# Two transformer blocks on one core: fill chunks, fin steps and index scores put in other places

## The reference

```
u = rmsnorm(h, mix_norm)
(fq, fk, fv, ff, dq, dk, dv, iq, ik, iw, mq, g) = split(u @ w_in)
o_a = fox_attention(fq, fk, fv, logf)             # 8 heads of 64, causal, with forget gates
score = sum_h iw_h * relu(iq_h . ik)              # index scores; top 128 keys for each query
o_b = dsa_attention(dq, dk, dv, ...)              # 8 heads over the chosen keys
km, vm = split(rmsnorm(mem, mem_norm) @ w_mem_kv)
o_c = memory_attention(mq, km, vm)                # 4 heads of 128 over 256 memory rows
gates = sigmoid(g)                                # 3 x 1024 columns
h = h + sum(gates * (branches @ w_branch)) @ w_out
```

## Time and profile before

| | |
|---|---|
| median of 3 runs | 2127.72 us (2126.78 to 2128.96) |
| profiled execution | 2127.72 us, its span 2125.9 us |
| TensorE busy | 1991.0 us, 94% |
| weight loads | 1613.4 us, 76% |
| GpSimd busy | 1450.9 us, 68% |
| VectorE busy | 977.3 us, 46% |
| ScalarE busy | 512.3 us, 24% |
| mean granted TensorE clock | 0.978 |

### The profile page before, as it was taken

How to read it: one execution, slowest core, us unless ns; L and a number is a source line. 1 busy time by engine, 2 the same in 40 slices (tenths; PEclk the granted TensorE clock), 3 DMA queues, 4 the chain that set the end, 5 groups by cost and what they waited for, 6 DMA issues and landing times.

```text
span 2125.9 us, 26050 instructions
## 1 busy us (share of the span) xinstructions
PE 1991.0 (94%) x8941; PEld 1613.4 (76%) x8941; DVE 977.3 (46%) x1198; ACT 512.3 (24%) x920; POOL 1450.9 (68%) x1662
## 2 busy tenths in 40 slices
PE   7999999999999989889999999999898879999996
PEld 6788888777777877777788888876677648888884
DVE  6432330687655477656432331057766573333004
ACT  3111100343444422430211110023555331111001
POOL 5777777776665656447777777776555568777771
PEclk9999999999999999999999999999999979999998
DMA  5333322332211223003333332242100113333320
GB/s 173 89 97 91 98 99 89 84 86 72 60 50 51 69 70 90 11 24 96 89 97 92 98 99 99 94 104 50 30 21 21 40 40 99 99 92 95 99 89 40
DMA packets 255460, 163.87 MB, mean 77 GB/s; under 512 B 30124, under 2 KB 245230, under 8 KB 255262
## 3 DMA queue, kind: packets, MB, share of 16 engines
q1 hardware_dynamic: 253728, 157.90, 25.4%
q10 hardware_dynamic: 1662, 5.06, 0.6%
HBM read 160.81 MB, written 2.13 MB: 77 GB/s over the span
## 4 chain that ended last, share of the span: by engine, by line
PE 76%; DVE 12%; POOL 6%; issue 3%; ACT 2%; DMA 1%; ACTq 0%; POOLq 0%; DVEq 0%; SPq 0%
PE bank L797 12%; PE bank L798 12%; PE bank L799 12%; PE bank L885 5%; PE bank L886 5%; PE bank L887 5%; PE bank L1056 4%; PE bank L1057 4%; PE bank L1058 4%; POOL w_lo L654 3%; PE bank L952 2%; DVE work L2309 1%; DVE work L2239 1%; POOL w_hi L650 1%; PE bank L1317 1%
## 5 line engine op out<-in xcount | busy, mean ns | idle before, releaser
L654 POOL TENSOR_TENSOR w_lo<-raw,w_hi 128x256 fp32r<-128x256 f32 x1192 | 953.9, 831 | 24.8
L650 POOL TENSOR_SCALAR w_hi<-raw 128x1024 fp32r<-128x1024 f32 x298 | 322.9, 1084 | 420.0 <-PE bank L799 165.1
L797 PE MATMUL bank<-u_hi,w_hi 128*128 128x512 f32 x1056 | 417.1, 395 | 16.9 <-DVE u_lo L2165 15.7
L798 PE MATMUL bank<-u_lo,w_hi 128*128 128x512 f32 x1056 | 413.8, 392 | 0.0
L799 PE MATMUL bank<-u_hi,w_lo 128*128 128x512 f32 x1056 | 413.6, 392 | 0.0
L797 PEld LDWEIGHTS bank<-u_hi,w_hi 128*128 128x128 f32 x1056 | 199.7, 189 | 66.4 <-issue 18.4
L799 PEld LDWEIGHTS bank<-u_hi,w_lo 128*128 128x128 f32 x1056 | 199.9, 189 | 42.2
L798 PEld LDWEIGHTS bank<-u_lo,w_hi 128*128 128x128 f32 x1056 | 200.1, 189 | 41.1 <-issue 0.7
L1056 PE MATMUL bank<-u_hi,w_hi 128*128 128x512 f32 x464 | 193.8, 418 | 2.3 <-DVE u_lo L2165 1.6
L885 PE MATMUL bank<-hid_hi,w_hi 128*128 (+1 forms) x480 | 187.0, 389 | 1.0 <-POOL w_lo L654 1.0
L887 PE MATMUL bank<-hid_hi,w_lo 128*128 (+1 forms) x480 | 186.8, 389 | 0.0
(11 more groups left out here) (513 smaller groups left out, 3263.4 us busy)
## 6 DMA issues: line engine op xcount, KB each, us to landing
raw<-in_w_in SPq DMA_DIRECT2D x52, 512.0 KB, 3.7
raw<-in_ffn_w_gate SPq DMA_DIRECT2D x44, 512.0 KB, 3.7
raw<-in_ffn_w_up SPq DMA_DIRECT2D x44, 512.0 KB, 3.8
raw<-in_ffn_w_down SPq DMA_DIRECT2D x44, 512.0 KB, 3.5
raw<-in_w_gate SPq DMA_DIRECT2D x22, 512.0 KB, 3.7
raw<-in_w_up SPq DMA_DIRECT2D x22, 512.0 KB, 3.7
...
```

The lines of the kernel that those rows point to most:

```text
L650: pool.tensor_scalar(w_hi[:, s, :], raw[:, k, :], 1.0, 1.0, ALU.mult, ALU.mult).then_inc(hi_done, 1)
L654: pool.tensor_tensor(w_lo[:, s, c], raw[:, k, c], w_hi[:, s, c].bitcast(F32), ALU.subtract).then_inc(low_quarter if quarter < 3 else split ...
L797: pe.matmul(outs[:, 0:n], wh, rhs_hi[:, c, :], start=(c == 0), stop=False)
L798: pe.matmul(outs[:, 0:n], wh, rhs_lo[:, c, :], start=False, stop=False)
```

## The change

It keeps all computation and moves it.

- Preparation. TensorE asks for the norm's total in unit DK instead of FG; the transposes of v go to bank 6 and to unit FG, the head sums of q0 and dk trade their banks. VectorE and ScalarE follow: the k split comes ahead of the v split, the head norm of q0 ahead of the FG copy.
- `fin` writes two work tiles in SBUF (`W[3]`, `W[4]`) instead of banks 2 and 6, and `fin_low` reads them there. The last steps (`fin_low` 4 to 7, `fin` 6 and 7) and the IQ0 copy move from memory slot 0 into `prep`.
- Memory slots. Of the filling steps, 1 instead of 3 stand behind the first score and 4 instead of 2 behind the last; 4 instead of 8 ahead of the value products.
- Fox slots. One step instead of two behind the first and the third score, two instead of one behind the third and fourth transposed score. ScalarE does `q_high` and the output copies ahead of the fifth `exps`; GpSimd splits unit u+4 between the sixth and the seventh low part.
- Gates. The index scores stand in gates 4 to 7 instead of 5 to 8.

TensorE at the start of memory slot 0, before: `L952` are its scores, `bank4` the chunks of the next panel.

```diff
--- before.py
+++ after.py
@@ -608,7 +608,6 @@
         I_BANKS = 0, 1, 6
         MEM_BANKS, FOX_BANKS = ((0,), (2, 3), (6,), 7), ((0,), (2, 3), (6, 7), None)
         AUX, Q_BANK, K_BANK = 1, 4, 5
-        FIN_BANKS = 2, 6
         USUAL = S_BANKS, T_BANKS, O_BANKS, DEN_BANK
         B2_BANKS = (0,), (2, 3), (6, 7), None
         FIRST_FILL = 7
@@ -620,7 +619,6 @@
 
             steps = [x for x, n in enumerate(n for head in FILLS for n in head) for _ in range(n)]
             return steps[k - FIRST_FILL]
-        IDX_GATES = range(5, 9)
         DQ_SUMS, DQ_TURNS = (9, 13, 17, 21), (11, 15, 19, 23)
         PV_LAG = 2
 
@@ -725,10 +723,12 @@
                     for k in (1, 2, 3):
                         low_part(A_FOX, fox_heads, steps[8 * p + k])
                     one(u + 3)
-                    for k in (4, 5, 6, 7):
+                    for k in (4, 5):
                         low_part(A_FOX, fox_heads, steps[8 * p + k])
-                    for k in (4, 5):
-                        one(u + k)
+                    one(u + 4)
+                    for k in (6, 7):
+                        low_part(A_FOX, fox_heads, steps[8 * p + k])
+                    one(u + 5)
             for u in range(RAW):
                 one(u)
             run(RAW, U_PREP)
@@ -1072,23 +1072,23 @@
                         pe.wait_ge(f_out, 7)
                         head_sum(H_K0, 6, k0_sq, ones, MEM)
                 for c in chunks(U_DK, 2, *early):
-                    if c == 4:
-                        values(VR_MEM, AUX, v0_raw, MT)
+                    if c == 2:
+                        pe.wait_ge(f_out, 8)
+                        sum_total(N_MIX, 7)
                 for c in chunks(U_FG, 3, *early):
                     if c == 1:
-                        pe.wait_ge(f_out, 8)
-                        sum_total(N_MIX, 7)
+                        pe.wait_ge(h_std, H_K0 + 1)
+                        values(VR_MEM, 6, v0_raw, MT)
+                    if c == 4:
+                        head_sum(H_Q0, AUX, q0_sq, ones)
                 for c in chunks(U_IK, 5, *early):
-                    if c == 2:
+                    if c == 3:
                         pe.wait_ge(n_std, N_MIX + 1)
-                        head_sum(H_Q0, 7, q0_sq, ones)
-                    if c == 5:
-                        pe.wait_ge(s_lo, S_MEM + 1)
-                        head_sum(H_DK, AUX, dk_sq, blk64)
+                        head_sum(H_DK, 7, dk_sq, blk64)
                 pe.wait_ge(p_raw, 1)
                 for c in chunks(U_DV, 4, *early):
                     if c == 3:
-                        pe.wait_ge(h_std, H_DK + 1)
+                        pe.wait_ge(h_std, H_Q0 + 1)
                         pe.wait_ge(p_raw, 3)
                         for i in range(TT):
                             last = pe.transpose(bank[AUX][:, i * HD:(i + 1) * HD], fg_raw[0:HD, i * P:(i + 1) * P],
@@ -1190,12 +1190,12 @@
                     pe.wait_ge(r_sin, R_PREP + i - 1)
                 for qt in range(TT):
                     scores(i, qt)
-                    go_on(panels, 1 if qt else 3)
-                go_on(panels, 2)
+                    go_on(panels, 1)
+                go_on(panels, 4)
                 for h, k, kb, t, b in steps:
                     scores_t(h, k, kb, t)
                     go_on(panels, 2)
-                go_on(panels, 8)
+                go_on(panels, 4)
                 for h, k, kb, t, b in steps:
                     values_mm(h, k, kb, b)
                     go_on(panels, 4)
@@ -1218,7 +1218,7 @@
                     values_mm(h, i, kb, b)
                 for qt in range(TT):
                     scores(2 * p, qt)
-                    go_on(panels, 2 if qt % 2 == 0 else 1)
+                    go_on(panels, 1)
                 for qt in range(2):
                     scores(2 * p + 1, qt)
                     go_on(panels, 1)
@@ -1229,7 +1229,7 @@
                     go_on(panels, 1)
                 for k in (2, 3):
                     t_of(k)
-                    go_on(panels, 1)
+                    go_on(panels, 2)
                 for k in range(4):
                     v_of(k)
                     go_on(panels, 1)
@@ -1273,10 +1273,10 @@
                     if n < 8:
                         pe.wait_ge(g_raw, 4)
                     else:
-                        pe.wait_ge(g_sig, n - 7 if n < 12 else n - 3)
+                        pe.wait_ge(g_sig, n - 7)
                     for c in chunks(U_GATE + n, 2 + n % 4, *U):
-                        if n in IDX_GATES and c >= 2:
-                            index_score(2 * (n - IDX_GATES[0]) + (c - 2) // 3, 1 + (c - 2) % 3)
+                        if n < 8 and c >= 2:
+                            index_score(2 * (n - 4) + (c - 2) // 3, 1 + (c - 2) % 3)
                         if n in DQ_SUMS and c == 3:
                             head_sum(H_DQ + DQ_SUMS.index(n), 6, W[4], blk64)
                         if n in DQ_TURNS and c == 4:
@@ -1752,7 +1752,7 @@
 
             def fin_high(c):
                 act.wait_ge(fin_t, c + 1)
-                act.activation(u_hi[:, c, :], bank[FIN_BANKS[c % 2]][:], ACT.Copy).then_inc(fin_hi, 1)
+                act.activation(u_hi[:, c, :], W[3 + c % 2], ACT.Copy).then_inc(fin_hi, 1)
 
             def prep():
                 act.wait_ge(unit_done, U_K0 + 1)
@@ -1760,22 +1760,22 @@
                 copy(k0_raw[:], bank[0][:, 0:MEM], h_raw)
                 head_std(H_K0, 6, k0_sq, P, MEM)
                 value_copy(U_V0, 1, v0_raw, MEM)
-                act.wait_ge(v_t, VT_MEM + 1)
-                copy(mst["vh"][:], bank[AUX][:, 0:MEM].rearrange("p (k n) -> p k n", k=MT), s_hi)
                 norm_std(N_MIX, b=7)
                 act.wait_ge(h_out, H_K0 + 1)
                 copy(mst["kh"][:], k0_raw[:], s_hi)
+                act.wait_ge(v_t, VT_MEM + 1)
+                copy(mst["vh"][:], bank[6][:, 0:MEM].rearrange("p (k n) -> p k n", k=MT), s_hi)
                 act.wait_ge(p_raw, 1)
                 act.activation(q0_sq[:], q0_raw[:], ACT.Square).then_inc(h_sq, 1)
                 act.wait_ge(p_raw, 2)
                 act.activation(dk_sq[:], dk[:], ACT.Square).then_inc(h_sq, 1)
                 fin_high(0)
-                head_std(H_Q0, 7, q0_sq, P)
+                head_std(H_Q0, AUX, q0_sq, P)
                 fin_high(1)
-                head_std(H_DK, AUX, dk_sq, HD)
-                load_exp()
                 act.wait_ge(h_out, H_Q0 + 1)
                 copy(mst["qh"][:], q0_raw[:], s_hi)
+                head_std(H_DK, 7, dk_sq, HD)
+                load_exp()
                 for c in range(2, 5):
                     fin_high(c)
                 act.wait_ge(iw_t, 1)
@@ -1934,12 +1934,11 @@
                     k_std()
                     forget_sums(p + 1)
                     load_exp()
+                    q_high()
                 else:
                     gate_copy(1)
+                output(2 * p)
                 exps(*steps[4])
-                if p < 3:
-                    q_high()
-                output(2 * p)
                 exps(*steps[5])
                 if p < 3:
                     v_copy()
@@ -1977,9 +1976,9 @@
 
             def later_gates():
                 for n in range(4, 24):
-                    if n in IDX_GATES:
+                    if n < 8:
                         for k in range(6):
-                            x = 6 * (n - IDX_GATES[0]) + k
+                            x = 6 * (n - 4) + k
                             cols_ = (2 + k % 3) * P
                             act.wait_ge(ix_s, x + 1)
                             if x >= 3:
@@ -2460,30 +2459,29 @@
             def fin(c):
                 if c >= 2:
                     dve.wait_ge(fin_lo, c - 1)
-                dve.scalar_tensor_tensor(out=bank[FIN_BANKS[c % 2]][:], in0=hT[:, c, :], scalar=gain[:, G_MIX + c:G_MIX + c + 1],
+                dve.scalar_tensor_tensor(out=W[3 + c % 2], in0=hT[:, c, :], scalar=gain[:, G_MIX + c:G_MIX + c + 1],
                                          in1=W[2], op0=ALU.mult, op1=ALU.mult).then_inc(fin_t, 1)
 
             def fin_low(c):
                 dve.wait_ge(fin_hi, c + 1)
-                dve.tensor_tensor(u_lo[:, c, :], bank[FIN_BANKS[c % 2]][:], u_hi[:, c, :].bitcast(F32), ALU.subtract).then_inc(fin_lo, 1)
+                dve.tensor_tensor(u_lo[:, c, :], W[3 + c % 2], u_hi[:, c, :].bitcast(F32), ALU.subtract).then_inc(fin_lo, 1)
 
             def prep_raw(u, dst_, b, r=P):
                 dve.wait_ge(unit_done, u + 1)
                 dve.tensor_tensor(dst_, bank[b][0:r, :], W[2][0:r], ALU.mult).then_inc(p_raw, 1)
 
             def prep():
-                low(S_MEM, mst["vl"][:], bank[AUX][:, 0:MEM].rearrange("p (k n) -> p k n", k=MT), mst["vh"][:])
                 head_norm(H_K0, k0_sq, k0_raw, G_MK, MEM)
                 norm_recip(N_MIX)
                 dve.wait_ge(n_rec, N_MIX + 1)
                 prep_raw(U_Q0, q0_raw[:], 4)
```

(17 more changed lines are left out.)

## The result

The changed kernel took 2145.56 us in the median (2145.09 to 2146.89, 4 runs) against 2127.8 before: the ratio is 1.0085, with a 95% interval of 1.0066 to 1.0102, so +17.8 us. Slower was forecast, but +9.3, and the time lies 3 us above the stated range. The profiled execution's span grew from 2125.9 to 2143.4, +17.5.

The account below looks back on a forecast made before the run. TensorE, busy 94% of the span, was taken as the bound, so only its waits matter. Memory slots and preparation +7.0, fox slots +1.4, gates -0.4 and clock +1.3 gave +9.3, 2137.0 us; range 2126 to 2142.5.

Parts of the forecast that it names:

- preparation, the wait for ik: Preparation: the norm's total is asked for five chunks earlier, so TensorE's 0.7 us wait for ik goes, -0.7.
- slot 0 (front 2.2, values 1.4): Memory slot 0: second score waits 2.2 us for the row maximum; value product waits for GpSimd's low part, +1.4.
- slot 3: Memory slot 3: second score +0.7; second head sum, now behind the value product, delays the fox scores, +1.6.
- A wash: Fox slots, third value product: GpSimd's 4.0 us split ends about when ScalarE releases the low part; -0.2 each in slots 0 to 2.
- The front's +0.7: Fox slots 1, 2 and 3: second score directly behind the first waits for the row maximum, 0.7 us each.
- Between -1.7 and +5; I take +1.3: Clock: new TensorE waits bring stretches at the lower clock, the one behind slot 2 may go; +1.3 taken.
- swallowed: Memory slot 2: its +2.1 falls ahead of the 2.43 us wait for the turned key, which absorbs it; net -0.3.
- Slot 0's front: Memory slot 0, second score: fin steps now precede the first row maximum, so TensorE waits 0.7 to 2.6 us, 2.2 taken.
- Moved, not removed: Gates: the 5.56 us wait at dq's rotation moves to before the first index score, about 6.2 us; -0.4 in all.
- the other side: Rival, 15%: the 5.6 us rotation wait and its 1.7 of clock are really given back, -7.3; kernel at 2124.
- the waits were not taken up: Judges the rival, 15%, that slots 0, 1 and 3 absorb the new waits as slot 2 does; 2130.
- the clock case: Rival, 10%: each of six new waits brings a lower-clock stretch of 1.7, +10 instead of +1.3; 2146.

Follow-up runs that it names:

- e_actpool: Kernel before with ScalarE's and GpSimd's new orders of the fox slots, filling steps as before; ratio to the kernel before 1.0022.
- e_foxact: Kernel before with only q_high and the output copies put ahead of the fifth exponential on ScalarE in the fox slots; ratio 0.9995.
- e_foxpool: Kernel before with only GpSimd's split of unit u+4 put between the sixth and seventh low part in the fox slots; ratio 1.0002.
- c_memback: Changed kernel with the memory slots' filling steps as before; 10.5 us under the changed kernel, ratio to the kernel before 1.0035.
- e_values: Kernel before with only 4 filling steps instead of 8 ahead of the memory slots' value products; ratio 1.0020.
- e_gates: Kernel before with only the index scores moved to gates 4 to 7; ratio 0.9995.

## Why the prediction was right in kind and wrong in size

Its own terms, in us, against the two traces; the stretches at the lower clock are taken out of the slots and stand in a line of their own:

| term | forecast | measured | missed by |
|---|---|---|---|
| preparation, the wait for ik | -0.7 | -1.1 | -0.4 |
| slot 0 (front 2.2, values 1.4) | +3.6 | +4.3 | +0.7 |
| slot 1 | +2.1 | +2.3 | +0.2 |
| slot 2 | -0.3 | +0.9 | +1.2 |
| slot 3 | +2.3 | +2.6 | +0.3 |
| fox slots | +1.4 | +4.1 | +2.7 |
| gates | -0.4 | +0.5 | +0.9 |
| clock, up to the gates | +1.3 | +4.1 | +2.8 |
| ahead of the preparation, behind the gates | 0 | -0.3 | -0.3 |
| sum | +9.3 | +17.5 | +8.2 |

The measured terms are rounded, and each comes from one execution of either kernel. The preparation runs from the first product on `e_hi` to slot 0's first score (41.69 against 42.76). The 0.72 by which the gates' edit shortens f3 stands under gates, and the +0.5 there is -0.1 by the means above. Measured clock: 2.4 in slot 0 (three scores and seven chunks took 7.9 us where 5.5 are their time at full clock) and 1.7 each in slots 1, 2 and fox slot 0, 7.5, against two of 1.7 before.

**Fox slots, the step "A wash".** This step failed. It laid the split (4.0 us) between two low parts and found that it ends when ScalarE releases the next. It used ScalarE's old times for the start, though the same paragraph moved ScalarE's work, and 4.0 for a split that took 4.68. e_actpool gives +0.7 to +0.8 in each of slots 0 to 2 in place of -0.2, and e_foxact with e_foxpool show that there either order alone gains. The front's +0.7 was right (+0.77); in slot 0 the front gave -0.8 where -0.4 was taken.

**The clock, the step "Between -1.7 and +5; I take +1.3".** The range held, the value did not. Slot 0's stretch was expected but got no price of its own and cost 2.4; that of slot 2 stands behind the 1.72 us wait that had been priced at 0.7, that of fox slot 0 behind two waits of 0.85 and 0.64 close together. c_memback supports the tie to the memory slots' waits; the fox slots' stars show that a part of it is chance.

**Slot 2, "swallowed".** The wait for the turned key did shrink, 2.43 to 0.48. But the front was priced at 0.7, from slot 1, where VectorE has nothing between; in slots 2 and 3 it is 1.7, because the key's last step and the low part of v stand ahead of the maximum. In slot 3 that was made up by the second head sum: in the changed kernel it leaves waits of 0.18 and 0.85 and not 1.6. With the values alone (e_values) slot 3 does grow by the 1.6 of the forecast, 32.39 against 30.78.

**Slot 0's front.** 3.4 against the upper end of 2.6: the last two fin_low took 1.33, not 0.76. By the rule of the Trainium skill (SBUF — State Buffer, "Who interferes with whom") a fin_low with two SBUF inputs contends with a GpSimd instruction that reads SBUF; the trace agrees in direction only. While GpSimd made the low part of one panel (427.21 to 431.76), one fin_low took 0.68 at 428.19 and the next 1.23 at 429.93, so the rule alone does not set the price.

**Gates.** Moved, not removed, as forecast, and the rival on the other side fell with e_gates. One premise was wrong: the head norm of dq does not end at the same time. The first rotation comes 2.8 us later behind the first index score (56.5 against 53.6), since the scores that it hangs on are slowed. That this is made up elsewhere, 0.7 us ahead of the index scores and 1.6 to 2.9 behind the rotation, where the slowed stretch is gone, makes the near hit (-0.1 by the means, -0.4 forecast) partly luck.

The rivals: the waits were not taken up; of the other side nothing was seen; the clock case (2146) had the right time with half of its mechanism: three new stretches, one of them of 2.4, less one, make 4.1 us and not 10, and the rest came from the fox slots.
